# Residual loads in halves around the weight fetches, second norms ahead of first norms, and another order in the latent attention of a two-block transformer kernel

## The reference

```python
def first_block(...):
    h = _rmsnorm(x, norm_gain); proj = h @ w_in
    ...
    x = x + mixed @ w_out
    return _rmsnorm(x, final_norm_gain)

def second_block(...):
    u = rmsnorm(h, g_pre); proj = u @ w_in
    y_a = rwkv7_branch(...)
    y_b = mla_branch(...)      # causal softmax attention, 8 heads, o * silu(z), @ w_out_b
    merged = sigmoid(gate_a) * y_a + sigmoid(gate_b) * y_b
    h = h + rmsnorm(merged @ w_o, g_post)
```

## Time and profile before

| | |
|---|---|
| median of 3 runs | 1915.79 us (1915.75 to 1918.11) |
| profiled execution, its own time | 1918.34 us |
| its span | 1916.5 us |
| PE busy | 1835.8 us (96%) |
| DVE, ACT, POOL busy | 954.0, 791.7, 417.1 us |
| mean granted TensorE clock | 0.992 |

### The profile page before, as it was taken

One profiled execution on the slowest core, in us unless ns is written; L12 is line 12 of the kernel. 1 busy time (PEld: TensorE's weight loads), 2 busy tenths in 40 slices (PEclk: granted clock), 3 DMA queues, 4 the chain that ended last, 5 costly groups with the idle time before them and its releaser, 6 DMA issues.

```text
span 1916.5 us, 37166 instructions
## 1 busy us (share of the span) xinstructions
PE 1835.8 (96%) x15473; PEld 1482.5 (77%) x15473; DVE 954.0 (50%) x2056; ACT 791.7 (41%) x1725; POOL 417.1 (22%) x416
## 2 busy tenths in 40 slices
PE   6999999999999999999999999999999999999998
PEld 6997766888886779777777778777777785667887
DVE  5677766243345244124554555544653346774523
ACT  5346666343445233233433334333432246554421
POOL 4550000121114331222222222222221301001321
PEclk9999999999999989999999999999999999999999
DMA  5153310323332422321211222212113220004442
GB/s 187 44 174 88 86 32 1 124 89 116 109 93 88 154 77 91 102 88 53 60 60 59 71 62 65 78 53 85 60 46 93 75 82 26 1 1 165 154 154 88
DMA packets 144751, 159.81 MB, mean 83 GB/s; under 512 B 14948, under 2 KB 123816, under 8 KB 144584
## 3 DMA queue, kind: packets, MB, share of 16 engines
q1 hardware_dynamic: 144360, 156.44, 25.5%
q0 software_dynamic: 224, 0.99, 0.2%
HBM read 110.53 MB, written 52.62 MB: 85 GB/s over the span
## 4 chain that ended last, share of the span: by engine, by line
PE 82%; DVE 5%; ACT 5%; POOL 3%; DMA 3%; issue 2%; SPq 0%; POOLq 0%; DVEq 0%; ACTq 0%
PE ps L985 8%; PE ps L695 7%; PE ps L987 7%; PE ps L986 7%; PE ps L696 7%; PE ps L697 7%; PE ps L1096 4%; PE ps L805 3%; PE ps L784 3%; PE ps L792 3%; PE ps L1133 3%; PE ps L1282 2%; PE ps L884 2%; PE ps L885 2%; PE ps L886 2%
## 5 line engine op out<-in xcount | busy, mean ns | idle before, releaser
L2765 POOL TENSOR_TENSOR t<-t,t 128x512 fp32r<-128x512 f32 x183 | 240.6, 1327 | 871.4 <-ACT t L1383 830.8
L985 PE MATMUL ps<-t,t 128*128 128x512 f32 (+2 forms) x720 | 293.4, 407 | 3.6 <-issue 2.3
L695 PE MATMUL ps<-t,t 128*128 128x256 f32 (+2 forms) x880 | 286.2, 325 | 2.8 <-DVE t L1958 1.3
L696 PE MATMUL ps<-t,t 128*128 128x256 f32 (+2 forms) x880 | 280.4, 319 | 0.0
L697 PE MATMUL ps<-t,t 128*128 128x256 f32 (+2 forms) x880 | 280.2, 318 | 0.0
L987 PE MATMUL ps<-t,t 128*128 128x512 f32 (+2 forms) x720 | 270.3, 375 | 0.0
L986 PE MATMUL ps<-t,t 128*128 128x512 f32 (+2 forms) x720 | 269.6, 374 | 0.0
L695 PEld LDWEIGHTS ps<-t,t 128*128 128x128 f32 x880 | 168.2, 191 | 20.0 <-issue 8.4
L697 PEld LDWEIGHTS ps<-t,t 128*128 128x128 f32 x880 | 168.1, 191 | 10.7
L696 PEld LDWEIGHTS ps<-t,t 128*128 128x128 f32 x880 | 168.2, 191 | 10.2 <-issue 0.2
L985 PEld LDWEIGHTS ps<-t,t 128*128 128x128 f32 x720 | 137.2, 191 | 32.6 <-issue 9.9
(11 more groups left out here) (271 smaller groups left out, 3261.8 us busy)
## 6 DMA issues: line engine op xcount, KB each, us to landing
t<-in_w_in SPq DMA_DIRECT2D x53, 512.0 KB, 5.9
zgate_spill<-t SPq DMA_DIRECT2D x20, 512.0 KB, 3.2
tile_bias<-t SPq DMA_DIRECT2D x16, 576.0 KB
t<-tile_bias SPq DMA_DIRECT2D x8, 1152.0 KB, 6.1
t<-in_x SPq DMA_DIRECT2D x16, 512.0 KB, 9.5
t<-zgate_spill SPq DMA_DIRECT2D x16, 512.0 KB, 4.4
feat_spill<-t SPq DMA_DIRECT2D x13, 512.0 KB, 3.2
tile_bias<-band_bias SPq DMA_DIRECT2D x48, 128.0 KB
```

What stands on the lines that cost most here:

```text
L695: e.matmul(dst, lh, rh, start=k == 0, stop=False)
L696: e.matmul(dst, lh, rl, start=False, stop=False)
L985: e.matmul(dst, lh, rh, start=k == 0, stop=False)
L2765: e.tensor_tensor(WLO[wslot(b)][:, o], WST[:, o], WHI[wslot(b)][:, o].bitcast(F), ALU.subtract).then_inc(w_lo.sem, w_lo.up((b, p)))
```

## The change

1. Sync engine: the residual tiles are loaded as sixteen halves of 256 KB. Eight (columns 0 to 511) go ahead of the fetch of block 15, the two gains between the fetches of 15 and 16, eight (columns 512 to 1023) behind the fetch of the first block of `w_in_2`. ACT and POOL split block 14 in one piece, and attention b no longer ends behind that.
2. PE enters block 16 without waiting for it as a whole and waits for each quarter in front of its use in tile 0.
3. Norms: in iteration i, n2 of tile i - 1 comes before n1 of tile i, on ACT, DVE and POOL.
4. Latent attention: ACT copies items n - 2 and n - 1 together, at even n, ahead of the exponential of n; DVE masks item n before it copies the first half of n - 2; value products 5 to 7 move from step 1 to step 2 and keep to banks 5 to 7; the weight pieces on ACT move to steps 9 and 17, tanh and output splits by one to six steps.
5. PE makes three quarters of the first merge group in steps 64 to 66, and three of the second right behind.
6. ACT splits `YA` tiles 1 to 3 in the second half of merge block 0, DVE tiles 2 and 3 at the start of block 1.

```diff
-            def enter():
+            def enter(whole=True):
                 wt.enter()
                 b = wt.b
-                if b:
+                if b and whole:
                     w.wait_ge(*w_hi[b, wlast(b)])
...
-            parts = [enter(), enter()]
+            parts = [enter(), enter(whole=False)]
+            def last_parts(x, i):
+                if i == 0:
+                    w.wait_ge(*w_hi[OUT1 + 3, x - 4])
+                    w.wait_ge(*w_lo[OUT1 + 3, x - 4])
...
+            def first_merge(half, k, hi, lo):
+                key = ("mg", 0, 0, half)
+                ps = bank_at(key, half, (merge_v, (0, 0, half, "gate"))) if k == 0 else psum(key)
+                latent_split(k, half)
+                e.matmul(ps, hi[:, k, 0:128], YBH[:, k, half512(half)], start=k == 0, stop=False)
...
+                if n == 64:
+                    hi, lo = enter()
+                    wt.ahead()
+                    first_merge(0, 0, hi, lo)
+                elif n > 64:
+                    first_merge(0, n - 64, hi, lo)
                 if 2 <= n < 66:
                     latent_turn(n - 2)
...
+            for k in range(3):
+                first_merge(1, k, hi, lo)
```

ACT, in the norms and in the latent attention:

```diff
-                w.wait_ge(*resid_v[1, i])
-                norm_square("n1", i, XR[:, i, :], JK2[:, :], 24)
                 if i:
                     w.wait_ge(*norm_v["final", i - 1])
                     norm_square("n2", i - 1, XR[:, i - 1, :], JK2[:, :], 48)
+                w.wait_ge(*resid_v[1, i])
+                norm_square("n1", i, XR[:, i, :], JK2[:, :], 24)
...
+                if 4 <= n < 66 and n % 2 == 0:
+                    turned_items(n - 2)
...
-                if n == 6:
+                if n == 9:
                     wt.leave(UQ)
-                elif n == 13:
+                elif n == 17:
                     wt.fetch_next()
                     wt.split(True)
...
-                    if x < 2:
-                        j = 2 * x + c
+                    for j in ((0,), (1, 2, 3))[c] if x == 0 else ():
```

The sync engine:

```diff
             wt.enter()
-            for _ in range(3):
-                wt.tick(12)
             for q in EVERY:
                 w.wait_ge(*q["attention b"])
-            for i in range(NT):
-                tile_load(XR[:, i, :], xv[i], i, "residual")
+            def load_residuals(g):
+                for i in range(NT):
+                    tile_load(XR[:, i, half512(g)], xv[i][:, half512(g)], i, ("residual", g))
+            load_residuals(0)
+            for _ in range(NT):
+                wt.tick(12)
+            wt.leave()
```

More of the change, by code:

```diff
@@ L948, in pe_program @@
                 for s, (hi, lo) in enumerate(parts):
-                    half_product("wo1", 1, s, i, hi, lo)
+                    half_product("wo1", 1, s, i, hi, lo, ready=last_parts if s else None)
                 if 1 < i:
@@ L1338, in pe_program @@
                         key = ("mg", x, c, half)
+                        if (x, c) == (0, 0):
+                            first_merge(half, 3, hi, lo)
+                            continue
                         ps = bank(key, ALL, (merge_v, (x, c, half, "gate")))
@@ L1608, in act_program @@
             band_part(3, 1)
-            for _ in range(2):
+            ACTE.end("attention b")
+            for _ in range(1, NT):
                 wt.tick(12)
-            ACTE.end("attention b")
+            wt.leave()
             for q in EVERY:
                 w.wait_ge(*q["attention b"])
-            for s in range(2):
-                if s:
-                    wt.enter()
-                for i in range(0 if s else 3, NT):
-                    wt.tick(12)
-                wt.leave()
+            wt.enter()
+            for _ in range(NT):
+                wt.tick(12)
+            wt.leave()
             wt.enter()
@@ L1855, in spread_sums, with turned_items @@
                 e.activation(RSB[x % 2].rearrange("p (s c) -> p s c", s=2), bc(RIN[:, c:c + 3:2], 2, 64), ACT.Copy).then_inc(lat_a.sem, lat_a.up(("sums", x)))
+            def turned_items(m):
+                for x in (m, m + 1):
+                    z = M_Z + x
+                    wd, _, _, pt = m_place(x)
+                    half = (wd - 1) // 512
+                    w.wait_ge(*prob_tr[z, half])
+                    if x >= 4:
+                        w.wait_ge(*value_mm["latent", (x - 4) // 4 * 2 + x % 2])
+                    e.activation(pt[:, 512 * half:wd], psum(("t", z, half))[:, 0:wd - 512 * half], ACT.Copy).then_inc(prob_hi.sem, prob_hi.up((z, half)))
             for n in range(64 + 5):
@@ L2863, in pool_program @@
                                     ALU.subtract).then_inc(band_lo.sem, band_lo.up(("b", p, r)))
-            for _ in range(3):
+            POOL.end("attention b")
+            for _ in range(NT):
                 wt.tick(12)
-            POOL.end("attention b")
+            wt.leave()
             for q in EVERY:
                 w.wait_ge(*q["attention b"])
-            for s in range(2):
-                if s:
-                    wt.enter()
-                for i in range(0 if s else 3, NT):
-                    wt.tick(12)
-                wt.leave()
+            wt.enter()
+            for _ in range(NT):
+                wt.tick(12)
+            wt.leave()
             wt.enter()
```

91 lines of the change are left out of this document (48 added, 43 removed).

## The result

The changed kernel takes 1895.06 us (median of 4 runs, 1894.22 to 1895.30) against 1916.39 us for the kernel before (4 runs, 1915.75 to 1918.11). The ratio is 0.9886, 95% interval 0.9873 to 0.9898: 21.3 us less, where 18.3 were forecast.

A forecast was written before the change was run, and what follows sets the result against it. The prediction took TensorE (PE), busy 96% of the span, as the bound. Projection and norms 13.6, latent attention 3.7 and YA splits 1.0 sum to 18.3 us, so 1915.79 - 18.3 = 1897.5 us, range 1892 to 1905.

The forecast's parts named there:

- Part 1: Output projection: earlier fetch of blocks 15 and 16 removes PE's stop, -5.0 us, and the low clock after it, -2.1 us.
- A: Rival: small residual loads run one behind the other, so block 15 lands late; gain only 13.4 us, 1902.4; 7%.
- E: Rival: the halves change nothing, block 15's fetch still comes late and the stop moves; gain 11.2 us, 1904.6; 3%.
- Part 2: Norms: n2 ahead of n1 removes PE's stops, -1.9 us, the low clock, -1.8, and small stops, -2.8.
- Rival B: DVE becomes the bound in the norms and their stops stay; gain 11.8 us, 1904.0; 9%.
- (a): Latent attention, first wide items: item 2's scores ahead of the second group of value products remove PE's wait, -1.1 us.
- (b): Latent attention, wait of 1.75 us at 1599.21: moving ACT's pieces to step 9 shortens it, -1.0 us.
- (c): Latent attention, each round of 16 items: copies ahead of the exponential, -0.5 us per round, -2.0 in four.
- (d): End of latent attention: three early merge groups fill PE's last waits, gain nothing, may delay the last transposes, +0.4 us.
- C: Rival: the latent order brings nothing, copies costing at middle items what they give elsewhere; gain 14.6 us, 1901.2; 8%.
- D: Rival: slower, each even latent exponential now waits for PE's transposes; +16.1 us, 1931.9; 3%.
- Part 4: Third merge block: earlier YA splits let POOL's two pieces take 2.55 us instead of 3.60, shortening PE's wait, -1.0 us.

The follow-up runs named there:

- halves_front: Changed kernel with all sixteen residual halves loaded ahead of the fetch of block 15: 1895.79 us, ratio 0.9882 to the kernel before.
- fetch_old: Changed kernel with residuals loaded as eight whole tiles ahead of both fetches and PE waiting for whole block 16, as before: 1902.29 us, ratio 0.9918.
- dve_two_more: Changed kernel with each of DVE's two low-half operations per tile in the norms done twice: 1899.05 us, ratio 0.9904.
- steps_old: Changed kernel with the latent attention's old first steps on PE and old steps for weight pieces, gates and output splits: 1897.46 us, ratio 0.9893.
- copies_old: Changed kernel with only the latent attention's copies of transposed items back in their old places on ACT and DVE: 1899.97 us, ratio 0.9904.
- halves_front_whole: Changed kernel with all sixteen residual halves ahead of the fetches and PE waiting for whole block 16 before starting block 15: 1897.75 us, ratio 0.9901.
- ya_old: Changed kernel with the YA splits of ACT and DVE spread over the first two merge blocks as before: 1897.18 us, ratio 0.9893.

## Why the prediction was right, and where its sizes were off

**The sum.** Forecast 18.3 us, measured 21.3 by the medians. By the profiles it is 23.3, and the stretches say of what: 0.5 lie ahead of the edits, 15.0 in the norms (forecast 13.6), 1.5 between the norms and the latent stretch, where nothing was changed, 4.7 in the latent attention (forecast 3.7), 1.6 at the third merge block (forecast 1.0). The 0.5 and the 1.5 are the execution's: in the second profile of the kernel before they are -0.3 and 0.8. The stretch at 841.55, with its low clock, took 15.19 us in the first, 13.65 in the second and 13.90 in the changed kernel's profile, which is 1.3 of the 1.5. The edits' own stretches give 15.0 + 4.7 + 1.6 = 21.3 us with the first profile of the kernel before, and 13.8 + 6.3 + 1.7 = 21.7 with the second (its norms had a shorter stop, 4.37 us, its latent attention a low clock behind a stop that the edits remove). Both agree with the medians. So the forecast missed by 3 us, and each part has its share.

**Part 1** (fetch). The forecast times of issue, landing and last piece hold within 0.6 us. The worst case of the working (data at 651.8, last piece at 668.6, wanted at 670.0) was met almost to the digit by halves_front, 651.66, 668.42 and 669.75, and no stop came of it, as forecast. Measured by fetch_old 8.0 us instead of 7.1. The term that was mis-sized is the clock's, 2.1: the window of 7.52 us ended before the tile did. Its 24 products took 7.77 us before (to 680.05) and 8.09 in fetch_old, against 5.44, so 2.3 and 2.7. The rest is the stop, 5.20 instead of 5.03, and what the next part says of stops. The reason given was the early landing first and the later need second; the runs show the second to be enough where the data land at 651.66, and whether it is so with the old loads wasn't run. Rivals A and E fall as to the time; A's reason, that small loads don't overlap, falls too, as block 15's data were there 7.4 us after the issue, not 21 us. The fit behind the 21 us stands in another section of that page of the Trainium skill than the one named (Anatomy of one DMA — SWDGE (gpsimd) path) and is for transfers that GpSimd issues; these are the sync engine's.

**Part 2** (n2 ahead of n1). 7.5 us instead of 6.5. The term that was mis-sized is the one of the small stops, three of 0.77 and one of 0.48, 2.8 us: a tile took 7.33 us before and 6.35 now, 0.98 less, where the shown wait was 0.77. About 0.2 us of each stop is hidden under the modelled end of the matmul before it (at full clock products of 128x512 start 0.23 us apart and are drawn 0.39 us long), which the text of the forecast's spread had named (0.15) but not put into the sum. Rival B falls, by 0.54 us a tile: had DVE needed 1.5 us more per tile, 3.1 of the 7.5 us would have gone (dve_two_more).

**Part 3** (latent attention). 4.7 instead of 3.7, and by stages it comes out otherwise than summed. Up to the first seventh item 3.2 us went (20.25 us from the load of the gates instead of 23.45), where (a), (b) and one round of (c) had 2.6; steps_old shows 2.2 for the 2.1 of (a) and (b), but not in the forecast's split, and (a) had the wrong condition: the wait goes only with the new copies too. Then three rounds gained 0.72 us each (0.65 by copies_old), not 0.5: the seventh item's wait went from 0.71 to 0.17 us (forecast 0.3 to 0.4), the next one from 0.35 to 0.38, the one behind it from 0.45 to 0.32, and the 0.18 us at the third item went as well, which I had not counted. Behind the last seventh item the changed kernel is 0.7 us longer (27.05 us to the end of the stretch instead of 26.35), as with steps_old, while copies_old has 26.36: there the new order of copies costs about what it gains in a round, and PE's last wait for an exponential is 0.77 us instead of 0.17. (d) I put at 0, with up to 0.4 lost. Nothing was lost, and in the one profile without the early products in which the clock fell there, it cost 1.5 us. Rivals C and D fall: in the rounds no wait of PE for an exponential or a copy is more than 0.03 us longer than before; only that last one shows the kind of wait that D was about.

**Part 4** (YA). Forecast 1.0, measured 1.1 by ya_old. The stretch gained 1.6 between the two profiles; the 0.5 beyond the edit is that ACT had its third gate 14.19 us behind the stretch's start instead of 14.69, and this time varies by more (13.55 to 14.65) among kernels with the same code there. PE's wait there was put at 2 to 3 us and came out at 1.63, since the whole stretch got shorter by 1.6: 1.21 before, 2.04 more by the early products, less 1.6.

## What to carry to other kernels

Put an engine's wait for a block in front of the block's first use, not in front of other work that doesn't need it: in halves_front that took away a stop of 2.34 us. Before adding up waits, measure the period of the repeating step, since each small stop cost about 0.2 us more here than the profile shows as idle. Between two profiles, lay stretches of unchanged code side by side first: what they differ by is not the edit's. And look what a stretch's end waits for: where it was not PE, a loss of 3.1 us looked like 5.6.

## What the runs showed of the hardware

The same stop of PE is followed by a low clock in one execution and not in another. Behind the latent attention's stop of 1.75 us the granted clock was 1.00 in one profile of the kernel before and 0.84 (over 10.60 us) in the other; behind the third merge block's it was 1.00 after 1.63 and after 2.82 us, and 0.85 after 1.95 us in copies_old (over 11.1 us); behind 2.34 us in halves_front_whole 1.00. Yet the stops of 1.88 us in the norms had a tile of 7.99 to 8.01 us behind them in all three profiles in which they occur. So the length of a stop doesn't tell whether the clock falls, and where it falls it costs 1.5 to 2.7 us here: about as much as the stop itself behind stops of 1.5 to 2 us. The prediction had called both of its stops long; among stops of 1.6 to 2.8 us the runs show no order by length.

The Trainium skill (TensorE: Matmul & The Clock Gate, Part 1: The HAM clock gate) calls the number of slow matmuls at a kernel's start variable from one run to the next. The trace shows the same behind stops in mid kernel, 1.00 against 0.84 behind the same 1.75 us.

A median over several executions averages this; a single profile doesn't. The two profiled spans differ by 2 us more than the medians do, and 1.3 us of it is the stretch at 841.55.
